# Two-layer hybrid backbone on one core: the later columns of w_ada as 64 bursts of 512 columns in the tiles ahead of attention and in layer 0's output stage, in place of 256 bursts of 128 on the heads' tiles

## The reference, cut to what matters

```python
mod = jax.nn.silu(cond) @ p['w_ada'] + p['b_ada']        # (2048) @ (2048 x 6144)
shift, scale, gate = jnp.split(mod[:, None, :], 3, axis=-1)
h = _rmsnorm(x, p['g_pre']) * (1 + scale) + shift
... = _split_proj(h, p['w_in'])      # heads: gated DeltaNet (4), latent attention (8), mLSTM (4)
y = jnp.concatenate([out_a, out_b, out_c], axis=-1) @ p['w_out']
x = x + gate * _rmsnorm(y, p['g_post'])
```

## Time and profile before

| | |
|---|---|
| Median of three runs | 3284.25 us |
| Span of the profiled execution (its own time) | 3284.9 us |
| PE busy | 3094.5 us (94%) |
| POOL busy | 2047.1 us (62%) |
| DVE busy | 1221.6 us (37%) |
| ACT busy | 831.4 us (25%) |
| PE on the bursts (L567) | 2048 instructions, 110.5 us busy |
| PE on the turns (L575) | 128 instructions, 17.0 us busy |
| Transfers for bursts | 256 of 256 KB |

### The profile page before, as it was taken

The page is one execution under the profiler, slowest core; times in us unless marked ns, Lnnn a source line. Parts: engine busy times, 40 slices in busy tenths (PEclk is TensorE's granted clock), DMA queues, the critical chain, the costliest instruction groups (busy, mean ns, idle before and its releaser), DMA issues. The chain is left out here.

```text
span 3284.9 us, 64747 instructions
## 1 busy us (share of the span) xinstructions
PE 3094.5 (94%) x27490; PEld 2791.5 (85%) x27490; DVE 1221.6 (37%) x2462; ACT 831.4 (25%) x1714; POOL 2047.1 (62%) x2491
## 2 busy tenths in 40 slices
PE   6899999999999999999997999999999999999996
PEld 1488888889999997879986888888999999787996
DVE  1255545532322113442117446655333312345112
ACT  1423433411111213331006324432111122233000
POOL 3273534446666887446877735544777888643886
PEclk9999999999999999999998999999999999999998
DMA  8533433424444221112223322321333222111322
GB/s 327 194 117 91 141 101 105 136 67 126 129 133 134 77 71 65 34 46 102 76 68 116 116 73 82 107 88 58 78 88 87 84 74 73 52 39 38 114 78 113
DMA packets 122034, 319.93 MB, mean 97 GB/s; under 512 B 18256, under 2 KB 27600, under 8 KB 120592
## 3 DMA queue, kind: packets, MB, share of 16 engines
q1 hardware_dynamic: 91008, 263.38, 25.3%
q10 hardware_dynamic: 30736, 52.40, 4.8%
HBM read 302.65 MB, written 13.08 MB: 96 GB/s over the span
## 5 line engine op out<-in xcount | busy, mean ns | idle before, releaser
L501 POOL TENSOR_SCALAR w_hi<-raw 128x256 fp32r<-128x256 f32 x1216 | 1050.8, 889 | 1171.6 <-PE projection L603 676.9
L508 POOL TENSOR_TENSOR w_lo<-raw,w_hi 128x256 fp32r<-128x256 f32 x1232 | 946.3, 799 | 6.3 <-ACT w_hi L1121 6.3
L601 PE MATMUL projection<-h_hi,w_hi 128*128 128x320 f32 x2304 | 763.8, 332 | 7.5 <-ACTq L1349 4.0
L603 PE MATMUL projection<-h_hi,w_lo 128*128 128x320 f32 x2304 | 715.0, 310 | 0.4 <-issue 0.3
L602 PE MATMUL projection<-h_lo,w_hi 128*128 128x320 f32 x2304 | 714.1, 310 | 0.5 <-issue 0.5
L548 PE MATMUL projection<-h_hi,w_hi 128*128 128x320 f32 x1984 | 616.3, 311 | 13.6 <-POOLq L513 11.4
L549 PE MATMUL projection<-h_lo,w_hi 128*128 128x320 f32 x1984 | 613.8, 309 | 0.0
L550 PE MATMUL projection<-h_hi,w_lo 128*128 128x320 f32 x1984 | 613.6, 309 | 0.0
L601 PEld LDWEIGHTS projection<-h_hi,w_hi 128*128 128x128 f32 x2304 | 435.9, 189 | 48.3 <-issue 41.8
L602 PEld LDWEIGHTS projection<-h_lo,w_hi 128*128 128x128 f32 x2304 | 436.6, 189 | 0.7 <-issue 0.7
L603 PEld LDWEIGHTS projection<-h_hi,w_lo 128*128 128x128 f32 x2304 | 434.8, 189 | 0.9 <-issue 0.9
(11 more groups left out here) (400 smaller groups left out, 4317.6 us busy)
## 6 DMA issues: line engine op xcount, KB each, us to landing
raw<-in_w_stream SPq DMA_DIRECT2D x308, 512.0 KB, 3.3
fill<-in_w_fill SPq DMA_DIRECT2D x256, 256.0 KB, 2.7
work<-in_w_ada SPq DMA_DIRECT2D x64, 512.0 KB, 4.9
work<-rows ACTq DMA_DIRECT2D x32, 320.0 KB, 4.0
xo<-rows ACTq DMA_DIRECT2D x32, 320.0 KB, 5.0
xo<-in_x ACTq DMA_DIRECT2D x1, 5120.0 KB, 16.9
work<-in_x ACTq DMA_DIRECT2D x16, 320.0 KB, 5.1
x_kept<-xo ACTq DMA_DIRECT2D x4, 1280.0 KB, 4.5
```

The lines of the kernel that those rows point to most:

```text
L501: nc.gpsimd.tensor_scalar(w_hi[:, s, cs, :], raw[:, s, cs, :], 1.0, None, ALU.mult).then_inc(split_part, 1)
L508: nc.gpsimd.tensor_tensor(w_lo[:, s, cs, :], raw[:, s, cs, :], w_hi[:, s, cs, :].bitcast(F32), ALU.subtract).then_inc(split_part, 1)
L601: mm(o, w_hi[:, half, c, :], h_hi[:, k, hs], start=(k == 0), stop=False)
L603: last = mm(o, w_lo[:, half, c, :], h_hi[:, k, hs], start=False, stop=(k == KT - 1))
```

## The change

The 64 column tiles are now 16 units of 512 columns. A unit has four bursts (one per quarter of the input tiles), each of four calls of 512 columns on four strips, and one turn of four column tiles. A burst needs a transfer of 1 MB into one of two `wide` slots. Bursts stand after the fourth cell of consecutive halves in `project`: 4 units in layer 0's tiles ahead of attention (layer 0's gate), 8 in layer 0's output stage (layer 1's shift and scale), 4 in layer 1's tiles ahead of attention (layer 1's gate). The turn stands after the fourth cell of the half behind a unit's last burst, or behind the stage for the last unit of the output stage. Units use the two banks of `wb` in turn, so the column sums for `ckv` move from `wb` to `wa`.

```diff
--- before.py
+++ after.py
+MLA_IN_AT = STREAM["gates"] + STREAM["gdn"] + STREAM["mlstm"]
+OUT_AT = STREAM_HALVES - STREAM["out"]
+
+
+def wide_plan():
+
+    gate = [(0, 8 + c, MLA_IN_AT + 10 + QUADS * c) for c in range(4)]
+    shift_and_scale = [(1, c, OUT_AT + QUADS * c) for c in range(8)]
+    last_gate = [(1, 8 + c, STREAM_HALVES + MLA_IN_AT + 10 + QUADS * c) for c in range(4)]
+    return gate + shift_and_scale + last_gate
+
+
+UNITS = wide_plan()
+GATE_UNITS = 4
+NORM_UNITS = 8
+
+BURST_AT = {at + q: (u, q) for u, (_, _, at) in enumerate(UNITS) for q in range(QUADS)}
...
+        def wide_bank(u):
+
+            return wb[:, (u % 2) * 512:(u % 2) * 512 + WIDE]
...
+            starts = sorted(BURST_AT)
             behind = {}
-            for i in range(len(BURSTS)):
-                n, k, _, _ = BURSTS[max(i - FILL_SLOTS, 0)]
-                behind.setdefault(n + k // CELLS + RAW_SLOTS, []).append(i)
+            for i in range(len(starts)):
+                behind.setdefault(starts[i - WIDE_SLOTS] + RAW_SLOTS if i >= WIDE_SLOTS else 8, []).append(i)
 
             for n in range(RAW_SLOTS, DEPTH * STREAM_HALVES):
                 stream(n)
                 for i in behind.get(n, ()):
-                    if i < FILL_SLOTS:
-
-                        sp.wait_ge(fill_ready, 1)
+                    if i < WIDE_SLOTS:
+
+                        sp.wait_ge(wide_room, 1)
                     else:
-                        sp.wait_ge(fill_free[i % FILL_SLOTS], i // FILL_SLOTS)
-                    sp.dma_start(fill[:, i % FILL_SLOTS, :, :].rearrange("p c n -> p (c n)"),
-                                 io["w_fill"][i, :, :]).then_inc(fill_full[i % FILL_SLOTS], 16)
+                        sp.wait_ge(wide_free[i % WIDE_SLOTS], i // WIDE_SLOTS)
+                    sp.dma_start(wide[:, i % WIDE_SLOTS, :, :].rearrange("p c n -> p (c n)"),
+                                 io["w_wide"][i, :, :]).then_inc(wide_full[i % WIDE_SLOTS], 16)
...
+                        if c == WIDE_CELL:
+                            if (n + half - 1) in BURST_AT and BURST_AT[n + half - 1][1] == QUADS - 1:
+                                wide_turn(BURST_AT[n + half - 1][0])
+                            if n + half in BURST_AT:
+                                wide_burst(*BURST_AT[n + half])
...
-            def burst(bank, i):
-
-                _, _, a, quad = BURSTS[i]
-                s = i % FILL_SLOTS
-                pe.wait_ge(fill_full[s], (i // FILL_SLOTS + 1) * 16)
+            def wide_burst(u, quad):
+
+                i = u * QUADS + quad
+                s = i % WIDE_SLOTS
+                if quad == 0 and u >= 2:
+
+                    pe.wait_ge(wide_added, u - 1)
+                pe.wait_ge(wide_full[s], (i // WIDE_SLOTS + 1) * 16)
                 for g in range(ROW_GROUPS):
-                    last = mm(bank[g * COND_W:(g + 1) * COND_W, a, HALF:HALF + P], cond[:, quad * ROW_GROUPS + g, :],
-                              fill[:, s, g, :], start=False, stop=(quad == QUADS - 1), skip_group_check=True)
-                last.then_inc(fill_free[s], 1)
-
-            def turn_rows(bank, tile):
-
-                pe.wait_ge(fill_taken, fill_taken_by(tile - 2))
-                for a in range(len(turned_in(tile))):
-                    mm(bank[:, a, HALF + P:HALF + P + 2], fill_rows[:, a, :], select,
-                       start=False, stop=True, skip_group_check=True)
+                    last = mm(wide_bank(u)[g * COND_W:(g + 1) * COND_W, :], cond[:, quad * ROW_GROUPS + g, :],
+                              wide[:, s, g, :], start=(quad == 0), stop=(quad == QUADS - 1))
+                last.then_inc(wide_free[s], 1)
+
+            def wide_turn(u):
+
+                pe.wait_ge(wide_copied, u + 1)
+                for c in range(WIDE_CELLS):
+                    last = mm(wide_bank(u)[:, 2 * c:2 * c + 2], wide_rows[:, c * P:(c + 1) * P], select,
+                              start=True, stop=True)
+                last.then_inc(wide_turned, 1)
...
-                        if (tile, k) in BURST_AT:
-                            burst(pj[j % 2], BURST_AT[tile, k])
-                        if k == SELECT_AT:
-                            turn_rows(pj[j % 2], tile)
...
                         B.wait("dve", "ckv squares")
-                        B.did(column_sums(wb, wt(7)), "ckv sum")
+                        B.wait("act", "cq rstd")
+                        B.did(column_sums(wa, wt(7)), "ckv sum")
                     if j == 12:
+                        B.wait("act", "ckv rstd")
...
                 M.wait("dve", "kv split")
+                pe.wait_ge(wide_added, GATE_UNITS if l == 0 else len(UNITS))
                 some_values(0, VALUE_TILES[0:2])
...
                     B.leave()
+                if l == 0:
+                    wide_turn(GATE_UNITS + NORM_UNITS - 1)
                 B = s_res.body("pe", pe, l)
...
-                tile = n + 2 * j
-                for a, (layer, at) in enumerate(turned_in(tile)):
-                    to = at + (KT if layer and at >= 2 * KT else 0)
-                    A(mod[:, to, :], pj[j % 2][:, a, HALF + P:HALF + P + 2], ACT.Identity,
-                      bias=bada[:, layer, at:at + 1]).then_inc(fill_taken, 1)
-                if tile in FILL:
-                    n = len(FILL[tile])
-                    A(fill_rows[:, 0:n, :], pj[j % 2][:, 0:n, HALF:HALF + P], ACT.Copy).then_inc(fill_taken, 1)
                 B.did(A(halves(dst), pj[j % 2][:, :, 0:HALF], ACT.Copy), f"ahead taken{j}")
...
+            def copy_wide(u):
+
+                for s in range(WIDE_SLOTS):
+                    dve.wait_ge(wide_free[s], (u + 1) * QUADS // WIDE_SLOTS)
+                V.tensor_copy(wide_rows[:, :], wide_bank(u)).then_inc(wide_copied, 1)
+
+            def add_wide(u):
+
+                layer, c, _ = UNITS[u]
+                at = c * WIDE_CELLS
+                to = at + (KT if layer and at >= 2 * KT else 0)
+                dve.wait_ge(wide_turned, u + 1)
+                V.tensor_tensor(mod[:, to:to + WIDE_CELLS, :],
+                                wide_bank(u)[:, 0:2 * WIDE_CELLS].rearrange("p (a b) -> p a b", b=2),
+                                bada[:, layer, at:at + WIDE_CELLS].unsqueeze(2).to_broadcast([P, WIDE_CELLS, 2]),
+                                ALU.add).then_inc(wide_added, 1)
...
+                first_unit = 0 if l == 0 else GATE_UNITS + NORM_UNITS
+                unit_behind = {7: first_unit, 8: first_unit + 1, 10: first_unit + 2, 12: first_unit + 3}
                 for j in range(7, 14):
+                    if j in unit_behind:
+                        copy_wide(unit_behind[j])
                     zb(j)
+                    if j in unit_behind:
+                        add_wide(unit_behind[j])
...
                     B.did(V.memset(cst[:, 2:3], 0.0), "begun")
+                    if l == 0 and f:
+                        copy_wide(GATE_UNITS + f - 1)
...
                         B.link(tt(wt(8), wt(8), wt(j), ALU.add))
+                        if l == 0 and f and j == 0:
+                            add_wide(GATE_UNITS + f - 1)
                     B.end()
+                if l == 0:
+                    copy_wide(GATE_UNITS + NORM_UNITS - 1)
+                    add_wide(GATE_UNITS + NORM_UNITS - 1)
...
-        nc = bacc.Bacc("TRN2", target_bir_lowering=False, num_devices=1)
+        nc = bacc.Bacc("TRN2", target_bir_lowering=False, num_devices=1, dynamic_dma_scratch_size=1024)
```

More of the change, by code:

```diff
@@ L56 @@
 QUADS = KT // ROW_GROUPS
-FILL_SLOTS = 2
+WIDE_SLOTS = 2
+WIDE = 512
+WIDE_CELLS = WIDE // P
+WIDE_CELL = 3
 HEADS_OF_VALUES = 4
-SELECT_AT = 13
 STREAM = dict(gates=2, gdn=8 * H_A, mlstm=10 * H_C, mla_in=30, mla=2 * H_B + H_B // HEADS_OF_VALUES, out=2 * KT)
@@ L193, in build @@
         raw = sb("raw", [P, RAW_SLOTS, CELLS, P])
-        fill = sb("fill", [P, FILL_SLOTS, ROW_GROUPS, P])
-        fill_rows = sb("fill_rows", [P, 2, P])
+        wide = sb("wide", [P, WIDE_SLOTS, ROW_GROUPS, WIDE])
+        wide_rows = sb("wide_rows", [P, WIDE])
         bada = sb("b_ada", [P, DEPTH, 48])
@@ L323, in flat_from @@
             return W[:, i:17, :].rearrange("p a n -> p (a n)")[:, at:at + n]
[L325 to L336, removed]
+        ada_rows = wide[:, 0, 0:2, :].rearrange("p g n -> p (g n)")
+        def wide_bank(u):
+            return wb[:, (u % 2) * 512:(u % 2) * 512 + WIDE]
         X_TILES = [2, 3, 6, 7, 9, 10, 11, 12, 13, 14, 15, 16, 0, 1, 8, 4]
@@ L388, in build @@
         ada_free = [sem(f"ada_free{s}") for s in range(ADA_SLOTS)]
[L389 to L392, removed]
+        wide_full = [sem(f"wide_full{s}") for s in range(WIDE_SLOTS)]
+        wide_free = [sem(f"wide_free{s}") for s in range(WIDE_SLOTS)]
+        wide_room = sem("wide_room")
+        wide_copied = sem("wide_copied")
+        wide_turned = sem("wide_turned")
+        wide_added = sem("wide_added")
         split_done = sem("split_done")
@@ L592, in cells @@
```

(10 more changed lines are left out.)

5 lines of the change are left out of this document (2 added, 3 removed).

## The result

The changed kernel takes 3255.4 us (median of four runs, 3254.5 to 3256.9) beside 3282.5 us for the kernel before (the median of four runs, three of which gave the 3284.25 us ahead of the prediction): ratio 0.9912, 95% interval 0.9893 to 0.9930. It is faster, by about 27 us, where 60 were forecast; the time lies 5 us above the range. The profiled executions say the same (span 3284.9 before, 3255.1 after).

The account below looks back on a forecast made before the run. PE issue was taken to bound the kernel: 155 us removed, 95 added (76 bursts, 14 turns, 3.5 copy waits, 1.2 layer end), so -60 and 3225 us. Its own range was 3205 to 3244, the stated range 3203 to 3250.

Parts of the forecast that it names:

- left to price: GDN heads, both layers: removing the 128 bursts and 32 turns that no layer difference shows saves 74 us.
- bursts in heads were not hidden under anything: GDN and mLSTM heads: each removed burst saves its PE time, about 0.55 us, as the layer differences showed.
- heads give some back: Rival, GDN heads: PE waits for DVE's chain instead; half of the 74 us lost, 3262 us; chance 0.10.
- The new burst: Output stage and tiles ahead of attention: eight passes in two rounds on four strips, 1.19 us net, 64 times, 76 us.
- passes in series: Rival, new bursts: five rounds instead of two, 1.31 us more each, 3309 us in all; chance 0.04.
- The wait for DVE's copy: Layer 0's output stage: PE waits about 0.5 us at the turn, seven times, 3.5 us (0 to 8).
- The layer's end: Layer 0's end: last unit's copy, turn, add and handovers take 2.1 us, 1.2 us beyond the turn already counted.
- transfers come late: Rival, output stage: 1 MB loads delay weight halves and starve POOL, 3240 us, up to 3255; chance 0.09.
- The mLSTM heads: Layer 0's second-branch heads: without bursts 322 us, as layer 1's, saving 41.6 us.
- The tiles ahead of attention: Both layers: 32 new bursts at 1.19 us and 8 turns at 0.88 us add 45.1 us.
- GDN heads of both layers about 435 us: Sign the forecast is right: first-branch heads take 472.10 us less some 37 in both layers.
- GDN heads with more idle time than before: Sign the forecast is wrong: PE idles longer in first-branch heads than 27.5 us (layer 0) and 24.6 (layer 1).

Follow-up runs that it names:

- the shorter chain: Two of four convolution multiply-adds left out for q and k in GDN heads: 3229.3 us on the changed kernel, 3279.9 us on the kernel before.
- PE waited five microseconds at the first block step: Changed kernel with 20 opening cells instead of 16 per GDN head, the four taken from the nine ahead of the block steps: 3286.4 us.
- unread products: Changed kernel with four products of 512 columns that nobody reads behind the 16 opening cells of each GDN head: 3256.4 us.
- the experiment with more cells: Changed kernel with 20 cells instead of 16 at each GDN head's opening, the four taken from the head's end: 3261.2 us.

## Why the prediction was wrong

**The step that failed** is the term "left to price": 74 us for the 128 bursts and 32 turns of the GDN heads "that no difference shows", on the ground that "bursts in heads were not hidden under anything". The ground came from the difference between the layers, 120 bursts against 64. That difference is a sound price for the first half of the bursts, since while there was slack at the opening, taking bursts out only made PE arrive sooner. It says nothing of the next half. By the prediction's own prices, all 184 bursts and 46 turns of the GDN heads are 151 x 0.55 + 33 x 0.24 + 46 x 0.22 = 101.1 us of PE. PE's busy time there fell by 99.9, so taken together these prices were right; its idle time rose by 21.4; 99.9 - 21.4 = 78.5, the measured gain. Of the 21.4, 21.1 are the wait for the square (1.8 us before, 22.9 after). So of the 35 us that are missing, 21.4 are PE's waits. 12.4 are price: 39.5 + 74 = 113.5 was more than the passes' 101.1, because I kept the measured 39.5 for 56 bursts and 14 turns, 8.4 above their passes (31.1 with nine of them at 0.24; the prediction's 33.9 took all at 0.55), and rounded the rest up by 4 from 70 with the mLSTM difference as the reason, where it spoke for the lower number.

**The rival named it** ("heads give some back") and was given 0.10. What I held against it was that the wait had fallen by 2.9 us between the layers. That was the wrong reading: a sum of waits over a stage says how much PE waits now, not how close the next wait is. The closeness was in the trace before: the square done 3.4 us ahead of PE in layer 0, about level in layer 1, with one wait of 1.8 us already there. Four bursts and a turned tile (4 x 0.55 + 0.22 = 2.4 us) fewer at the opening of layer 1 had to turn mostly into a wait; in layer 0 twice as much (4.8 us), less 3.4 us of slack, had to leave a wait of 1.4. It came out longer, 3.7. In the two heads above, PE's way to the sum fell by more than the prices, from 20.4 to 14.3 us (part of it because its first cells of before ran at 1.2 GHz, until 474.2), and the chain itself grew from 17.0 to 18.0: 3.4 - 6.1 - 1.0 = -3.7. The two stretches from first cell to square, after and then before, in the columns of the earlier trace rows:

```profile
333.01:350.98 17.97, 14.33 (x99) 14.06 (x97) 14.36 (x28) 10.99 (x18) 15.02 (x15) 1.00 0.25 78
473.12:490.07 16.95, 16.20 (x138) 13.38 (x138) 13.24 (x28) 10.99 (x18) 8.78 (x11) 0.97 0.54 172
```

DVE's same 28 instructions took 1.1 us more, and POOL was busy for 15.0 us of the stretch in place of 8.8: with PE earlier, POOL's splits lie over the chain. That the splits are what made DVE slower is likely (see the last section) but was not tested by itself.

**What was right.** The new burst: forecast 0.24 to free the array, 1.00 for two rounds, 0.25 to resume. Measured in the output stage:

```profile
1507.91 0.31 PE L537 MATMUL projection<-h_hi,w_lo 128*128 128x320 f32 x1
1508.15 1.06 PE L562 MATMUL wb<-wide,cond 128*32 128x512 f32 x8
1509.15 0.41 PE L535 MATMUL projection<-h_hi,w_hi 128*128 128x320 f32 x1
1509.40 0.31 PE L536 MATMUL projection<-h_lo,w_hi 128*128 128x320 f32 x1
```

0.24, 1.00 and 0.25, and a half with a burst takes 8.24 us where one without took 7.04 (forecast 1.19 more). The rival "passes in series" needed 1.31 us more per burst and is out. The Trainium skill's factor of 3.07 for four row tiles ("TensorE: Matmul & The Clock Gate", Part 3, measured speedup) would have made the 1.00 into 1.14 (an estimate); the trace does not agree. (By the prediction's own figures that would have been 0.14 us more a burst and 9 us in all, not the 0.27 and 17 that stand there.)

The wait for DVE's copy: forecast half a microsecond, seven times, from DVE's marker and a copy of 0.65 us. DVE and then PE in the output stage after the change:

```profile
1516.04 0.06 DVE L1962 MEMSET small_constants<- 128x1 f32 x1 [0.30 <-DVE work L1973]
1516.11 0.69 DVE L1504 COPY wide_rows<-wb 128x512 f32<-128x512 f32 x1
```

```profile
1516.86 1.05 PE L570 MATMUL wb<-constants,wide_rows 128*128 128x2 f32 x8 [0.40 <-DVE wide_rows L1504]
```

Copy 0.69, wait 0.40. The layer's end cost 2.0 us for 2.1. The transfers cost nothing: PE waits for none of the 64 loads of 1 MB and, in the output stage, for no weight half, nor does POOL wait there for a load, and the rival "transfers come late" is out. The mLSTM heads came to 321 us as said, 2.9 us better than the sum had them. The tiles ahead of attention cost 40.1 and not 45.1 us; most of that is luck, since PE's waits for POOL's split in `project` fell from 11.4 to 8.0 us, which the sum did not have.

Of the signs the prediction named, "GDN heads of both layers about 435 us" failed at 454 and 451, and "GDN heads with more idle time than before" is the one that came. With the chain shortened they take 437 and 440 us, and with the shorter chain in both kernels the change is worth 3279.9 - 3229.3 = 50.6 us of the 60: the passes had been priced about rightly, and what was missing was the question what stands behind them.

## What to carry to other kernels

Before pricing the removal of filler from a busy engine, measure the slack at each place that the filler precedes: when the producer is done, and when the waiter gets there. A difference between two stages prices a removal only as long as that slack lasts; summed waits do not show it. And where a chain of another engine has become the bound, that place is free room for other work, up to the wait's length, but moving the next steps there only moves the wait if they stood in front of the chain's later results.

## What the runs showed of the hardware that was not expected

- The granted clock fell behind waits. PE was at 1.2 GHz for 3.4 us behind an idle time of 3.70 us (352.10 above), for 23.9 us behind such waits in the GDN heads of the changed kernel, for 75.1 us in those heads where PE waited five microseconds at the first block step, for 6.8 where unread products filled the wait, and not at all with the shorter chain. What it costs is an estimate: PE's busy time for the same passes was 12.5 us longer with the long chain, beside 22.9 us of waits, so about half of a wait again.
- DVE and POOL were slower beside each other. POOL's four subtractions of a weight half took 4.15 us beside the convolution of k, and 2.80 elsewhere in the same kernel, where DVE stood idle for most of them:

```profile
345.21 4.15 POOL L495 TENSOR_TENSOR w_lo<-raw,w_hi 128x256 fp32r<-128x256 f32 x4
...
431.14 2.80 POOL L495 TENSOR_TENSOR w_lo<-raw,w_hi 128x256 fp32r<-128x256 f32 x4
```

  DVE's four multiply-adds took 4.40 us in that stretch and 3.69 just before it, where POOL was at the first half of its split. "Trainium Architecture — The Big Picture" of the Trainium skill (What this means for kernel authors) names a port pair that the two share, held by one at a time; the longer spans on both sides agree with that, but no run here tells it from a split of bandwidth. It may be why the 17th cell's weights came late in the experiment with more cells, since POOL's split lies beside the very chain that PE would be covering; that was not tested.
